# Moving the row product of the norm factors behind unit 2, and loading the first two modulation chunks at the start of a two-block transformer kernel

## The reference

```python
h = rmsnorm(x, norm_mix[i])                       # x * rsqrt(mean(x*x)) * gain, one factor per token
q, k, v = jnp.split(x @ w_in, [2 * H * dh, 4 * H * dh], axis=-1)   # in diff_attention; 6 chunks of 512 columns
q = rmsnorm(q.reshape(B, T, H, 2, dh), q_gain) * (dh ** -0.5)
k = rmsnorm(k.reshape(B, T, H, 2, dh), k_gain)
...
def _ada(cond, w_ada, b_ada):                     # in the second block, for c and for c_ctx
    mod = jax.nn.silu(cond) @ w_ada + b_ada       # 1024 x 3072: 6 chunks of 512 columns
    return jnp.split(mod, 3, axis=-1)             # shift, scale, gate
```

## Time and profile before

| | |
|---|---|
| median of 3 runs | 961.28 us (960.3 to 961.59) |
| profiled execution, time | 961.18 us |
| its span, first to last instruction | 959.1 us |
| mean granted clock | 0.993 |
| PE busy | 925.4 us (96%) |
| DVE, ACT, POOL busy | 349.2, 217.8, 124.9 us |

### The profile page before, as it was taken

The page is one execution under the profiler, slowest core; times in us unless marked ns, Lnnn a source line. Parts: engine busy times, 40 slices in busy tenths (PEclk is TensorE's granted clock), DMA queues, the critical chain, the costliest instruction groups (busy, mean ns, idle before and its releaser), DMA issues.

```text
span 959.1 us, 13033 instructions
## 1 busy us (share of the span) xinstructions
PE 925.4 (96%) x5404; PEld 505.0 (53%) x5404; DVE 349.2 (36%) x789; ACT 217.8 (23%) x474; POOL 124.9 (13%) x123
## 2 busy tenths in 40 slices
PE   7899799989999999999999999999999999999998
PEld 3488565434555553333333333334588888755543
DVE  2564422345774462001110110127635542354422
ACT  2122212334554411010010010113301111642310
POOL 3202202000000211000000000023201312340000
PEclk9999899999999999999999999999999999999999
DMA  9913477504201437999999999972193102600002
GB/s 330 284 18 119 149 259 263 242 1 174 90 1 44 163 114 290 394 378 405 426 403 427 422 414 414 384 274 72 51 177 107 63 23 83 220 1 2 1 12 77
DMA packets 54235, 186.34 MB, mean 194 GB/s; under 512 B 13968, under 2 KB 14624, under 8 KB 47904
## 3 DMA queue, kind: packets, MB, share of 16 engines
q1 hardware_dynamic: 45776, 160.31, 44.9%
q0 software_dynamic: 4912, 18.36, 5.2%
q10 hardware_dynamic: 3488, 6.82, 1.9%
HBM read 168.70 MB, written 16.79 MB: 193 GB/s over the span
## 4 chain that ended last, share of the span: by engine, by line
PE 87%; DVE 6%; DMA 2%; ACT 2%; POOL 2%; issue 1%; ACTq 0%; DVEq 0%; SPq 0%; POOLq 0%
PE psum L902 19%; PE psum L1104 17%; PE psum L1127 8%; PE psum L813 6%; PE psum L1259 6%; PE psum L1004 6%; PE psum L951 5%; PE psum L928 5%; PE psum L965 2%; PE psum L982 2%; PE psum L1315 1%; PE psum L1031 1%; PE psum L1221 1%; PE psum L865 1%; POOL qk_st L2466 1%
## 5 line engine op out<-in xcount | busy, mean ns | idle before, releaser
L1104 PE MATMUL psum<-ring,buf_a 128*32 128x512 f32 x1536 | 167.5, 593 | 1.1 <-DVE buf_a L2158 1.1
L1104 PEld LDWEIGHTS psum<-ring,buf_a 128*32 128x32 f32 x1536 | 48.9, 110 | 110.2 <-issue 110.2
L1127 PE MATMUL psum<-ring,buf_c 128*32 128x512 f32 x768 | 84.7, 594 | 0.0
L902 PE MATMUL psum<-ring,buf_a 128*128 128x256 f32 x320 | 71.5, 381 | 0.0
L2466 POOL TENSOR_TENSOR qk_st<-qk_st,half 128x8 f32<-128x8 f32 x26 | 43.6, 1677 | 172.9 <-DVE qk_st L2238 71.4
L902 PEld LDWEIGHTS psum<-ring,buf_a 128*128 128x128 f32 x320 | 60.0, 190 | 10.3 <-issue 2.5
L902 PE MATMUL psum<-ring,buf_b 128*128 128x256 f32 x288 | 65.2, 382 | 0.0
L1004 PE MATMUL psum<-ring,buf_b 128*128 128x512 f32 x128 | 59.8, 594 | 0.0
L902 PEld LDWEIGHTS psum<-ring,buf_b 128*128 128x128 f32 x288 | 54.3, 191 | 9.5 <-issue 2.5
L1826 DVE TENSOR_TENSOR s_buf<-s_buf,psum 128x512 f32<-128x512 f32 x52 | 35.3, 685 | 65.4 <-PE psum L902 60.3
L1259 PE MATMUL psum<-ring,buf_b 128*128 128x512 f32 x128 | 56.2, 595 | 1.7 <-DVE buf_b L2436 1.5
(11 more groups left out here) (304 smaller groups left out, 1192.5 us busy)
## 6 DMA issues: line engine op xcount, KB each, us to landing
ring<-in_moe_w_gate SPq DMA_DIRECT2D x16, 2048.0 KB, 11.1
ring<-in_moe_w_up SPq DMA_DIRECT2D x16, 2048.0 KB, 12.7
ring<-in_moe_w_down SPq DMA_DIRECT2D x16, 2048.0 KB, 11.9
ring<-in_w_in SPq DMA_DIRECT2D x7, 2048.0 KB, 9.5
ring<-in_w_ada SPq DMA_DIRECT2D x6, 2048.0 KB, 8.4
ring<-in_da_w_in SPq DMA_DIRECT2D x5, 2048.0 KB, 20.3
y_d<-ring POOLq DMA_DIRECT2D x1, 5632.0 KB, 22.1
y_d<-buf_b ACTq DMA_DIRECT2D x11, 512.0 KB, 11.2
```

Source lines behind the costliest of these rows:

```text
L902: last = mm(out_bank[:, a * 256:(a + 1) * 256], still, moving, start=(k == 0), stop=(k == KD // 2 - 1))
L1104: last = mm(buf("mm", n)[rows, :], xgT[:, s % 4, k, rows], slot(moe_load(q, m, r))[:, k, :], start=(k == 0), stop=(k == KD - 1))
L1127: last = mm(buf("sc", n)[rows, m, :], hidT[:, s % 3, f * P + SUB * j:f * P + SUB * (j + 1)], slot(moe_load(q, 2, r), FC)[:, f, m * CH:(m + ...
```

## The change

The row product L937 is issued after unit 2 instead of after unit 1. The modulation chunks 0 and 1 are loaded at the start into slots 4 and 5. The value weights, which had these slots, come later: chunk 4 when the rows of modulation chunk 0 are done, chunk 5 when those of chunk 1 are. The rows and column sums of chunks 0, 1 and 2 move to earlier products (q1 4 and 6, k0 1 and 3, k0 6 and 7), chunks 3 to 5 keep their places. Each modulation chunk has a semaphore of its own.

```diff
@@ -65,10 +65,9 @@
 
 
 ADA_CHUNKS = 6
-ADA_ROWS_BEHIND = {("k0", 4): 0, ("k0", 7): 1, ("k1", 2): 2, ("k1", 4): 3, ("k1", 6): 4, ("unit", 16): 5}
-ADA_BEHIND = {("k0", 6): 0, ("k1", 1): 1, ("k1", 3): 2, ("k1", 5): 3, ("k1", 7): 4, ("unit", 17): 5}
-ADA_SLOT = [1, 1, 1, 2, 1, 2]
-ADA_TURN = [1, 2, 3, 1, 4, 2]
+ADA_ROWS_BEHIND = {("q1", 4): 0, ("k0", 1): 1, ("k0", 6): 2, ("k1", 4): 3, ("k1", 6): 4, ("unit", 16): 5}
+ADA_BEHIND = {("q1", 6): 0, ("k0", 3): 1, ("k0", 7): 2, ("k1", 5): 3, ("k1", 7): 4, ("unit", 17): 5}
+ADA_SLOT = [4, 5, 1, 1, 2, 1]
 UNITS_FIRST = 18
 V_STEPS = 16
 
@@ -597,7 +596,7 @@
     second_loaded = sem("second_loaded")
     ctx_loaded = [sem(f"ctx_loaded{t}") for t in range(CT)]
     spills_done = sem("spills_done")
-    ada_landed = [sem(f"ada_landed{b}") for b in range(2)]
+    ada_landed = [sem(f"ada_landed{c}") for c in range(ADA_CHUNKS)]
     fold_ready = sem("fold_ready")
     gate_ready = sem("gate_ready")
     cond_ready = sem("cond_ready")
@@ -650,8 +649,16 @@
                     ks = slice(4 * b, 4 * b + 4)
                     sp.dma_start(ring[:, W_IN, :].rearrange("p (k n) -> p k n", k=KD)[:, ks, :],
                                  w_in[:, ks, 0:CH]).then_inc(first_landed if b == 0 else w_landed[W_IN], 16)
-        for c in range(1, 6):
+        w_ada = A["w_ada_2"][0].rearrange("(k p) n -> p k n", p=P)
+
+        def load_ada(c):
+            sp.dma_start(ring[:, ADA_SLOT[c], :].rearrange("p (k n) -> p k n", k=KD),
+                         w_ada[:, :, c * 512:(c + 1) * 512]).then_inc(ada_landed[c], 16)
+
+        for c in range(1, 4):
             load(W_IN + c, w_in[:, :, c * CH:(c + 1) * CH])
+        load_ada(0)
+        load_ada(1)
 
         with nc.allow_non_contiguous_dma(reason="small vectors laid along partitions"):
             sp.dma_start(cond[:, :, 0], A["c_2"][0].rearrange("(k p) -> p k", p=P)).then_inc(second_loaded, 16)
@@ -665,7 +672,6 @@
             sp.dma_start(mask[:], A["mask"]).then_inc(second_loaded, 16)
             sp.dma_start(chan[:], A["chan"]).then_inc(second_loaded, 16)
         w_out = A["da_w_out"][0].rearrange("(k p) n -> p k n", p=P)
-        w_ada = A["w_ada_2"][0].rearrange("(k p) n -> p k n", p=P)
 
         with nc.allow_non_contiguous_dma(reason="small vectors laid along partitions"):
             sp.dma_start(gain2[:], A["norm_ffn"][0].rearrange("(p k) -> p k", p=P)).then_inc(late_loaded, 16)
@@ -676,15 +682,18 @@
             sp.dma_start(w_rt[:, :, GROUPS:20], A["moe_w_router"][0].rearrange("(p k) g -> p k g", p=P)).then_inc(late_loaded, 16)
             sp.dma_start(b_rt[:, 0:GROUPS], A["moe_b_group"].broadcast_to([P, GROUPS])).then_inc(late_loaded, 16)
             sp.dma_start(b_rt[:, GROUPS:20], A["moe_b_router"].broadcast_to([P, EXPERTS])).then_inc(late_loaded, 16)
-        for c in range(ADA_CHUNKS):
-            if c == 0:
-                sp.wait_ge(product_done[0], 7)
-            elif c == 3:
-                sp.wait_ge(product_done[0], 14)
-            else:
-                filled(sp, "tp", turn["tp", "ada_rows", {1: 0, 2: 1, 4: 2, 5: 3}[c]])
-            sp.dma_start(ring[:, ADA_SLOT[c], :].rearrange("p (k n) -> p k n", k=KD),
-                         w_ada[:, :, c * 512:(c + 1) * 512]).then_inc(ada_landed[ADA_SLOT[c] - 1], 16)
+        filled(sp, "tp", turn["tp", "ada_rows", 0])
+        load(W_IN + 4, w_in[:, :, 4 * CH:5 * CH])
+        sp.wait_ge(product_done[0], 7)
+        load_ada(2)
+        filled(sp, "tp", turn["tp", "ada_rows", 1])
+        load(W_IN + 5, w_in[:, :, 5 * CH:6 * CH])
+        filled(sp, "tp", turn["tp", "ada_rows", 2])
+        load_ada(3)
+        sp.wait_ge(product_done[0], 14)
+        load_ada(4)
+        filled(sp, "tp", turn["tp", "ada_rows", 3])
+        load_ada(5)
         sp.wait_ge(product_done[0], 21)
         for c in range(2):
             load(W_OUT[c], w_out[:, :, c * CH:(c + 1) * CH])
@@ -858,7 +867,7 @@
                 claim(pe, "tp", n)
                 if c == 0:
                     pe.wait_ge(cond_ready, 1)
-                pe.wait_ge(ada_landed[ADA_SLOT[c] - 1], 16 * ADA_TURN[c])
+                pe.wait_ge(ada_landed[c], 16)
                 for r in range(2):
                     for j in range(4):
                         k = 4 * r + j
@@ -932,7 +941,7 @@
             fill(last, "mm", n)
             if 1 <= i < TT:
                 qk_transposes(i - 1)
-            if i == 1:
+            if i == 2:
                 pe.wait_ge(diag_ready, 1)
                 mm(bank(0, 0, 6), ones[:], part["c11"], start=True, stop=True).then_inc(rstd_row_ready, 1)
             work_behind("unit", i)
@@ -1772,7 +1781,7 @@
                 drain(V.tensor_tensor(gate_col[:, cols], buf("tp", n)[:, 0:8:2], added, ALU.add), "tp", n)
 
 
-        ada_in = {("k0", 7): 0, ("k1", 0): 1, ("k1", 2): 2, ("k1", 6): 3, ("k1", 7): 4}
+        ada_in = {("q1", 6): 0, ("k0", 2): 1, ("k0", 7): 2, ("k1", 6): 3, ("k1", 7): 4}
 
         def ada_sums(*place):
             if place in ada_in:
```

## The result

| | before | changed |
|---|---|---|
| median | 961.01 us (960.3 to 961.59, 4 runs) | 946.38 us (943.88 to 947.6, 4 runs) |
| ratio, 95% interval | | 0.9845 (0.9823 to 0.9866) |
| profiled execution, span | 961.18, 959.1 | 943.88, 941.8 |
| PE busy, mean granted clock | 925.4, 0.993 | 918.1, 1.000 |

The account below looks back on a forecast made before the run. The prediction took TensorE to bound the kernel, with 87% of the span PE work. Removed waits and slow matmuls, 5.84 + 8.08 = 13.9 us, brought 961.2 to 947.3 us, range 945.0 to 953.5.

Parts of the forecast that it names:

- Part 1: Row product behind unit 2: removes the 4.02 us wait for DVE's diagonals and slow matmuls after it, 5.84 us together.
- the term for the slow clock: First twelve matmuls of unit 2, slow behind the row product's wait: 5.75 us to become 5.15, gain 0.60.
- DVE's margin, 1.0 us before unit 3 ends: DVE's delayed scaling pieces finish at about 42.3 us, TensorE's unit 3 at 43.3, so TensorE need not wait.
- Part 2: End of k0 and k1 2: reordered modulation jobs remove two waits on DVE and slow matmuls, 8.08 us; loads alone nothing.
- One step of its margins: End of k0: third scaled block ready 12.9 us after product 5, TensorE reaches it after 17.2; margin 4.
- The sum: Both gains added, 5.84 + 8.08 = 13.9 us, taken from the profiled 961.2 us to give 947.3.
- The rest moves along: After the edited stage, all starts, including expert loads and clearing of y, hang on TensorE and move earlier with it.
- rival C: Expert stage: the weight stream takes the gain back, leaving 961 us; chance 0.04.
- Rival A's inner case: Attention, 1.80 us wait at 208.4: the clock fall behind it may not come, 945.4 us; chance about one in four.
- Rivals B and D: B: late DVE scaling or wrong buffer claim, 953.1 to 955.4, chance 0.15; D: q1 rows await condition vector, slower, 0.04.

Follow-up runs that it names:

- ada_early: The changed kernel with the row product back behind unit 1, so only the modulation loads and jobs come earlier; 951.09 us, ratio 0.9905.
- drain_early: The kernel before, with only DVE's additions of the column sums of chunks 0 and 1 made earlier; 951.87 us, ratio 0.9898.
- dve_late: The changed kernel with four unused DVE additions between the scalings of tiles 1 and 2; 946.96 us in one execution.
- drain_row: The kernel before with DVE's column-sum additions earlier and the row product behind unit 2, no load moved; 946.54 us, ratio 0.984.
- row_late: The kernel before with only the row product moved behind unit 2, modulation unchanged; 954.94 us, ratio 0.9927.
- changed_again: The changed kernel run once more without edits, for the spread between executions; 946.51 us, ratio 0.9844.
- dve_pool_meet: The changed kernel with five more unused DVE multiplications in the mixer, during POOL's output-weight multiplications; 948.69 us, ratio 0.9875.
- o_first: The changed kernel with DVE emptying the output buffer before the difference of softmaxes in attention step 10; 944.47 us, ratio 0.9824.

## Why the prediction was right

**Part 1, 5.84.** Right as a mechanism: wait 4.02 to nothing, row product 2.08 to 0.86, unit 2's twelve matmuls 5.75 to 5.15. Alone the part took 6.5 us out of the stage; 0.7 of that is that the rows and the product behind the second stall, which stays in this kernel, were slow for less long (3.32 and 3.65 against 3.64 and 4.06), which leaves 5.8. So the term for the slow clock depends on the execution: the twelve matmuls behind the same 4.02 us wait took 5.75 in the profile before, but 6.91 in ada_early's and 7.09 in drain_early's:

```profile
32.70 6.91 PE psum L937 x12
```

```profile
32.73 7.09 PE psum L928 x12
```

The term of 0.60 was taken from the cheapest of the three, and is 1.2 to 1.3 us too small beside the others.

**DVE's margin, 1.0 us before unit 3 ends.** In the changed kernel the scaling of tile 2 began at 39.62 and took 1.2, unit 3 ended at 41.9: 1.1. dve_late puts the cover of this place and the next block together at 2.0.

**Part 2, 8.08.** Its claim that the gain is the order at the end of k0, and that the loads by themselves give nothing, is shown by drain_early and drain_row: without a moved load the same ratio within the intervals. Both waits and the slow pieces behind the first went. Alone, part 2 took 7.26 us out of the stage in ada_early and 6.81 in drain_early; both profiles pay the dearer slow stretch behind the first stall, and with its 1.16 and 1.34 us added back it is 8.4 and 8.2. One step of its margins is added up wrongly: TensorE needs 17.4 us, not 17.2, to come to the third block of k0. The margin is 4 all the same.

**The sum.** 13.9 against 14.26 measured in the stage between two profiles. I took the waits from the modelled end of the last matmul: 4.02 in the timeline, but 31.57 - 27.40 = 4.17 from the moment at which the next matmul could have started. In part 1 this cancels: counted from start to start, the wait is 4.17, the row product 1.87 instead of 0.86, the twelve matmuls 5.79 instead of 5.15, together 5.8. In part 2 it does not: counted so, the two waits are 5.03 and 1.19 and the whole is 8.3. The last 0.1 lies in gaps too small for the list of waits, among them some 0.3 us at the block behind q1 7 in the kernel before.

**The rest moves along.** Shown: from unit 16 to the end 809.4 before, 807.3 to 810.6 in all the others (row_late's apart). It is 807.3 to 808.0 in the profiles in which the four matmuls behind the attention's wait took 1.98 us, and 809.3 to 810.6 in those in which they were slow. The weight stream of the experts took nothing back, so rival C falls.

**Rival A's inner case,** "14 us earlier that fall may not come", happened in the first profile and not in changed_again's. It isn't a matter of being 14 us earlier: the same kernel shows both. These two traces agree with the Trainium skill (TensorE: Matmul & The Clock Gate, "What's actually happening"), where it says that the monitor's window runs free of the kernel. I gave the case one in four; of the nine executions of the changed kernel three had a mean clock of 1.000.

**Rivals B and D** did not occur; both mechanisms were made to occur and cost 2.6 us (4.6 of added work) and 5.3 us, at the places named.

**Where the forecast was short by 1 us:** 0.3 of it is in the stage, as above. The rest is not located. It is small beside the spread of the changed kernel (943.9 to 947.6), and the slow stretches at the start and in the attention, outside the edited stage, differ between executions by 1.3 and 1.7 us, so that two medians agree with a sum to 1 us is in part luck.

## What to carry to other kernels

A wait for a double buffer can be a wait for the drain of an unimportant user two turns back. Look at what that user's drain is queued behind on its engine before moving loads; here one addition of 0.16 us, placed behind three scaled blocks, held TensorE for 4.87 us, and moving only such additions gave the same time as loading and computing the modulation earlier. A stall of TensorE is priced with the slow matmuls behind it, and that part varies between executions, so read it from several. Removing a wait of under 2 us can also pay more than its length: 0.9 us less here gave 2.0 between the medians, and the mean clock of all five executions says that the slow stretch no longer came.

## What was not expected of the hardware

**The clock fell behind a wait of 1.80 us in some executions only.** Ten of the eleven profiles have this same wait, whatever the edit ahead of it. The four matmuls behind it took 3.43 us before, 3.68 in changed_again, 3.31 in drain_row and 2.96 in dve_pool_meet, and 1.98 in the other six, the first profile of the changed kernel among them. The rows of drain_row and dve_pool_meet:

```profile
194.19 3.31 PE L951 MATMUL psum<-ring,buf_b 128*128 128x512 f32 x4 [1.80 <-DVE o_sb L1995]
```

```profile
193.94 2.96 PE L960 MATMUL psum<-ring,buf_b 128*128 128x512 f32 x4 [1.80 <-DVE o_sb L2003]
```

Behind 0.89 us they took 1.98 in the one profile of o_first, and its other four executions had the same mean clock of 1.000; behind 1.65 us in dve_late it did not fall either. Nothing tried here says which executions are spared: the edit does not decide it, since one kernel shows both.

**One DVE operation of 10.3 us instead of 1.2.** In row_late's profiled execution, some 800 us behind the edit, this row of DVE's timeline:

```profile
832.39 10.29 DVE L2423 TENSOR_TENSOR o_sb<-ident,rden 128x1024 f32<-128x1024 f32 x1
```

and TensorE's wait for it:

```profile
PE psum L1354 <- DVE o_sb L2423: 9.6, 1, 9.6
```

POOL was in its run of sixteen multiplications, which reads and writes SBUF:

```profile
821.91 19.69 POOL L2623 TENSOR_TENSOR ring<-ring,g_x 128x512 f32<-128x512 f32 x16 [22.40 <-DMA ring<-in_w_out]
```

It ended at 841.60, and DVE's operation, at 842.68, 1.08 us later, about what the operation normally takes. In the other ten profiles the same operation overlaps the same run and took 1.2 to 1.9 us, and POOL's run took 20.7 us (22.6 in dve_pool_meet, with its added operations), not 19.69, as here in the changed kernel:

```profile
812.99 20.70 POOL L2632 TENSOR_TENSOR ring<-ring,g_x 128x512 f32<-128x512 f32 x16 [22.41 <-DMA ring<-in_w_out]
```

In each of those ten at least one of POOL's operations took some 2.3 us instead of 1.28; in row_late's none did (1.27 to 1.29). So elsewhere POOL lost about 1 us to DVE, and here it lost nothing. The Trainium skill (SBUF — State Buffer, "Summary: rules for kernel authors") has a DVE instruction with two SBUF inputs and a POOL instruction that reads SBUF exclude one another, the later of the two blocked until the earlier is over; the four meetings in dve_pool_meet (0.6 to 1.1 us longer) agree, the 10.3 us do not, since they span some seven POOL instructions. Another execution of row_late (964.13) and one of the kernel before (970.71) were 9 us above their medians; whether for the same reason isn't known, as they have no trace. Why DVE was kept out over a whole run once stays open: the one experiment on it did not bring it back. It is no part of the change, and the medians hardly see it.
